# Reading attention's units on an expert-routed decoder trunk: one fused instruction for bias and maximum, factors by pairs, four logit banks, and unread TensorE products in waits

## What is computed

```python
lc = einsum(q, k_cmp) + bias;  pc = masked_softmax(lc)            # 15 compressed blocks
ls = einsum(q, k_slc) + bias;  ps = masked_softmax(ls)            # selected blocks
lw = einsum(q, k_win) + bias;  pw = masked_softmax(lw)            # window
out = g0 * (pc @ v_cmp) + g1 * (ps @ v_slc) + g2 * (pw @ v_win)   # gates per head
h = h + out @ w_out
logits = rmsnorm(h) @ w_router;  top_v, top_i = top_k(logits, 2)
h = h + sum over experts of gate_e * swiglu_e(rmsnorm(h))
```

## Time and profile before

| | us |
|---|---|
| time, median of 3 runs | 1418.52 (1417.91 to 1419.12) |
| profiled execution | 1417.83 |
| its span | 1416.2 |
| PE busy | 1368.9 (97%) |
| DVE busy | 430.5 (30%) |
| ACT busy | 306.0 (22%) |
| POOL busy | 148.9 (11%) |
| mean granted PE clock | 0.986 of full |

### The profile page before, as it was taken

How to read it: one execution, slowest core, us unless ns; L and a number is a source line. 1 busy time by engine, 2 the same in 40 slices (tenths; PEclk the granted TensorE clock), 3 DMA queues, 4 the chain that set the end, 5 groups by cost and what they waited for, 6 DMA issues and landing times.

```text
span 1416.2 us, 36112 instructions
## 1 busy us (share of the span) xinstructions
PE 1368.9 (97%) x16162; PEld 841.7 (59%) x16162; DVE 430.5 (30%) x621; ACT 306.0 (22%) x491; POOL 148.9 (11%) x223
## 2 busy tenths in 40 slices
PE   8999999999998889999999999999999999999995
PEld 7999999998985573453453443444344344344343
DVE  6986555556458730110110110110110110110120
ACT  6735534434457820000000000000000000000000
POOL 0600100000304714001001001001001001001001
PEclk9999999999998999999999999999999999999998
DMA  9853465555957079999999999999999999999993
GB/s 289 257 175 120 129 220 187 180 179 161 187 185 252 28 283 377 400 418 400 419 418 401 418 418 402 418 418 398 419 418 400 418 418 402 418 416 400 406 387 127
DMA packets 132305, 452.08 MB, mean 319 GB/s; under 512 B 12563, under 2 KB 74236, under 8 KB 132162
## 3 DMA queue, kind: packets, MB, share of 16 engines
q1 hardware_dynamic: 126386, 435.11, 79.3%
q0 software_dynamic: 5600, 14.62, 4.2%
q10 hardware_dynamic: 176, 0.14, 0.0%
HBM read 436.46 MB, written 11.80 MB: 317 GB/s over the span
## 4 chain that ended last, share of the span: by engine, by line
PE 93%; DVE 3%; ACT 2%; DMA 1%; issue 1%; POOL 1%; SPq 0%; POOLq 0%; ACTq 0%; DVEq 0%
PE ps L1691 92%; DVE arena L1522 1%; DVE arena L1525 1%; DMA ring<-in_a_w_in 1%; ACT x_hi L964 1%; POOL arena L826 0%; DMA arena<-item_rows,arena 0%; PE ps L1995 0%; ACT arena L1174 0%; ACT x_hi L994 0%; DVE w_lo L527 0%; PE ps L1803 0%; ACT w_hi L521 0%; ACT between L1201 0%; PE ps L1870 0%
## 5 line engine op out<-in xcount | busy, mean ns | idle before, releaser
L1691 PE MATMUL ps<-ring,arena 128*32 128x448 f32 (+1 forms) x3136 | 300.2, 536 | 1.6 <-DVE arena L1650 1.6
L1660 DVE TENSOR_TENSOR arena<-arena,ps 128x448 f32<-128x448 f32 x48 | 29.8, 621 | 755.1 <-PE ps L1691 751.0
L1691 PEld LDWEIGHTS ps<-ring,arena 128*32 128x32 f32 (+1 forms) x3136 | 104.4, 110 | 191.3 <-issue 185.5
L1691 PE MATMUL ps<-more,arena 128*32 128x448 f32 x1920 | 183.3, 539 | 0.0
L527 DVE TENSOR_TENSOR w_lo<-ring,w_hi 128x2048 fp32r<-128x2048 f32 x66 | 151.3, 2295 | 76.9 <-ACT w_hi L521 76.7
L1691 PE MATMUL ps<-more,between 128*32 128x256 f32 x2688 | 158.1, 379 | 0.0
L521 ACT ACTIVATE w_hi<-ring 128x2048 fp32r<-128x2048 f32 x66 | 125.7, 1910 | 93.2 <-PE ps L1691 88.2
L1691 PEld LDWEIGHTS ps<-more,arena 128*32 128x32 f32 x1920 | 62.6, 110 | 115.2 <-issue 113.8
L1691 PEld LDWEIGHTS ps<-more,between 128*32 128x32 f32 x2688 | 92.6, 110 | 53.2
L1245 ACT ACTIVATE arena<-ps 128x448 f32<-128x448 f32 x48 | 26.1, 544 | 413.2 <-PE ps L1691 413.2
L1691 PE MATMUL ps<-x_hi,w_hi 128*128 128x256 f32 x672 | 94.4, 291 | 7.0 <-ACT x_hi L964 5.0
(11 more groups left out here) (279 smaller groups left out, 1376.1 us busy)
## 6 DMA issues: line engine op xcount, KB each, us to landing
ring<-in_moe_w_gu SPq DMA_DIRECT2D x128, 896.0 KB, 19.9
more<-in_moe_w_gu SPq DMA_DIRECT2D x80, 896.0 KB, 19.7
more<-in_moe_w_down SPq DMA_DIRECT2D x64, 896.0 KB, 20.3
arena<-in_moe_w_down SPq DMA_DIRECT2D x32, 896.0 KB, 20.5
ring<-in_ffn_w_gu SPq DMA_DIRECT2D x22, 1024.0 KB, 5.0
ring<-in_a_w_in SPq DMA_DIRECT2D x16, 1024.0 KB, 11.5
silu_g<-in_moe_w_gu SPq DMA_DIRECT2D x16, 896.0 KB, 19.0
xn<-in_moe_w_gu SPq DMA_DIRECT2D x16, 896.0 KB, 19.7
```

What stands on the lines that cost most here:

```text
L1660: dve.tensor_tensor(SU[:, a, :], SU[:, a, :], ps[:, b, 0:QUARTER], ALU.mult).then_inc(bank_free[b], 1)
L1691: return pe.matmul(o, w, x, start=start, stop=stop, **kw)
```

## The change

In attention: one instruction (`tensor_tensor_reduce`) for each branch of a unit adds the bias, negates, and gives the minimum as second output; the exponential uses scale -1 to undo the sign. The exponential of the first branch may start when that branch is done. The factors are computed for two units at once, two units later than before (steps 3, 5, ...). DVE scales the first branch of every unit, POOL the second. From unit 8 on (HB // 2) the logits rotate over four banks, (4, 0, 1, 7)[u % 4]. The compressed branch of the second tile comes at step 8 instead of 12, in bank 6. And `pass_time` issues products of the identity with ones, 256 columns each, into a bank that the next job overwrites: 1, 2, 2, 3 and 3 of them at attention's start, 2 and 2 in the router.

```diff
--- before.py
+++ after.py
@@ -57,6 +57,7 @@
 BUCKETS, MAXDIST = 32, 2048
 COPIES = 16
 NEG = -1e30
+HUGE = 3.0e38
 
 E, ED = 8, 3584
 EK = ED // P
@@ -145,10 +146,6 @@
 def turned_with(u):
 
     return u - u % 2 if ORDER[u // HB] == 0 else u
-
-
-def both_on_pool(u):
-    return ORDER[u // HB] == 0 or u % 2 == 1
 
 
 def job_table():
@@ -214,11 +211,14 @@
     job(("kc",), 7)
     job(("vc",), 6)
     job(("kcsum",), 5)
-    for tt in ORDER:
-        job(("LC", tt), 7)
-        job(("PCT", tt), 7)
     for u in range(TT * HB):
-        job(("L", u), (0, 1, 4)[u % 3])
+        if u in (0, HB):
+            job(("LC", ORDER[u // HB]), 7 - u // HB)
+            job(("PCT", ORDER[u // HB]), 7 - u // HB)
+        if u < HB // 2:
+            job(("L", u), (0, 1, 4)[u % 3])
+        else:
+            job(("L", u), (4, 0, 1, 7)[u % 4])
         if turned_with(u) == u:
             job(("PT", u), 2 + (u // 2 if ORDER[u // HB] == 0 else u) % 2)
     for n in range(TT * 2):
@@ -609,7 +609,7 @@
             b, k = JTURN[name]
             return b, JBASE[b] + k + i * JPER[b]
 
-        CMP_AT = [4 + HB // 2 * ORDER.index(tt) for tt in range(TT)]
+        CMP_AT = [4 + HB // 4 * ORDER.index(tt) for tt in range(TT)]
         units = [(tt, h) for tt in ORDER for h in range(HB)]
 
         def pv_release(eng, u):
@@ -820,10 +820,9 @@
                 pool.dma_start(by_parity(KT, high, br, 0), by_parity(KT, low, br, 0)).then_inc(keys_copied, 16)
 
             for u, (tt, h) in enumerate(units):
-                pool.wait_ge(weight_ready, u + 1)
-                for br in (0, 1) if both_on_pool(u) else (1,):
-                    v = LB[:, u % KEPT, br, 0:P * (tt + 1)]
-                    pool.tensor_scalar(v, v, RW[:, u, br:br + 1], None, ALU.mult).then_inc(p2_ready, 1)
+                pool.wait_ge(weight_ready, u // 2 + 1)
+                v = LB[:, u % KEPT, 1, 0:P * (tt + 1)]
+                pool.tensor_scalar(v, v, RW[:, u, 1:2], None, ALU.mult).then_inc(p2_ready, 1)
 
             pool.wait_ge(counted, 1)
             steps = [0]
@@ -1168,10 +1167,13 @@
             for s in range(len(units) + LAG):
                 if s < len(units):
                     w = P * (units[s][0] + 1)
-                    act.wait_ge(row_max, s + 1)
                     for br in range(2):
+                        if br == 0:
+                            act.wait_ge(row_max, s + 1)
+                        else:
+                            evacuated(act, ("L", s))
                         v = LB[:, s % KEPT, br, 0:w]
-                        act.activation(v, v, ACT.Exp, bias=RM[:, s, br:br + 1], accum_out=RS[:, s, br:br + 1]).then_inc(exp_done, 1)
+                        act.activation(v, v, ACT.Exp, bias=RM[:, s, br:br + 1], scale=-1.0, accum_out=RS[:, s, br:br + 1]).then_inc(exp_done, 1)
                 if s == 0:
                     k = filled(act, ("kcsum",))
                     act.activation(kcsq, ps[:, k, 0:G * NCMP], ACT.Ln, bias=eps[:, :], scale=1.0 / DH).then_inc(bank_free[k], 1)
@@ -1183,11 +1185,6 @@
                     tt = CMP_AT.index(s)
                     act.wait_ge(pc_shift, ORDER.index(tt) + 1)
                     act.activation(PC[:, tt, :, :], PC[:, tt, :, :], ACT.Exp).then_inc(pc_exp, 1)
-                if 1 <= s <= len(units) and not both_on_pool(s - 1):
-                    u = s - 1
-                    act.wait_ge(weight_ready, u + 1)
-                    v = LB[:, u % KEPT, 0, 0:P * (units[u][0] + 1)]
-                    act.activation(v, v, ACT.Copy, scale=RW[:, u, 0:1]).then_inc(p_ready, 1)
                 if s >= LAG:
                     u = s - LAG
                     if units[u][0]:
@@ -1518,11 +1515,13 @@
                 k = filled(dve, ("L", s))
                 if s >= KEPT:
                     filled(dve, ("PT", turned_with(s - KEPT)))
-                lb = LB[:, s % KEPT, :, 0:w]
-                dve.tensor_tensor(lb, ps[:, k, 0:2 * w].rearrange("p (b t) -> p b t", b=2),
-                                  BD[:, h:h + 1, T - w:T].to_broadcast([P, 2, w]), ALU.add).then_inc(bank_free[k], 1)
-                evacuated(dve, ("L", s))
-                dve.reduce_max(RM[:, s, :], lb, AX.X, negate=True).then_inc(row_max, 1)
+                for br in range(2):
+                    last = dve.tensor_tensor_reduce(LB[:, s % KEPT, br, 0:w], ps[:, k, w * br:w * br + w], BD[:, h, T - w:T], -1.0, HUGE,
+                                                    ALU.add, ALU.min, RM[:, s, br:br + 1])
+                    if br == 0:
+                        last.then_inc(row_max, 1)
+                    else:
+                        last.then_inc(bank_free[k], 1)
 
             dve.wait_ge(bias_in, 16 * P // COPIES)
             for n in range(3):
@@ -1557,7 +1556,7 @@
                                               K("seen")[:, tt:tt + 1], wt, ALU.mult, ALU.mult))
                 dve.tensor_tensor(pc, pc, wt.unsqueeze(2).to_broadcast([P, HB, NCMP]), ALU.mult).then_inc(pc_ready, 1)
 
-            for s in range(len(units) + 1):
+            for s in range(len(units) + 2):
                 if s - 3 in CMP_AT:
                     tt = CMP_AT.index(s - 3)
                     k = filled(dve, ("PCT", tt))
@@ -1587,12 +1586,17 @@
                     cmp_scores(CMP_AT.index(s))
                 if s - 1 in CMP_AT:
                     cmp_weights(CMP_AT.index(s - 1))
-                if s >= 1:
-                    u = s - 1
+                if s >= 3 and s % 2 == 1:
+                    u = s - 3
                     tt, h = units[u]
-                    dve.wait_ge(exp_done, 2 * u + 2)
-                    link(dve.reciprocal(RW[:, u, :], RS[:, u, :]))
-                    dve.tensor_tensor(RW[:, u, :], RW[:, u, :], gates[:, tt, 3 * h + 1:3 * h + 3], ALU.mult).then_inc(weight_ready, 1)
+                    dve.wait_ge(exp_done, 2 * u + 4)
+                    link(dve.reciprocal(RW[:, u:u + 2, :], RS[:, u:u + 2, :]))
+                    by_head = gates[:, tt, 3 * h:3 * h + 6].rearrange("p (n b) -> p n b", b=3)
+                    dve.tensor_tensor(RW[:, u:u + 2, :], RW[:, u:u + 2, :], by_head[:, :, 1:3], ALU.mult).then_inc(weight_ready, 1)
+                    dve.wait_ge(weight_ready, u // 2 + 1)
+                    for n in range(2):
+                        v = LB[:, (u + n) % KEPT, 0, 0:P * (tt + 1)]
+                        dve.tensor_scalar(v, v, RW[:, u + n, 0:1], None, ALU.mult).then_inc(p_ready, 1)
             pv_release(dve, len(units) - 3)
             input_lo(OT)
             dve.wait_ge(rows_set, 16 * (E + 2 * T // TILE))
@@ -1984,10 +1988,8 @@
 
             def turned(u):
                 tt = units[u][0]
-                scaled = [both_on_pool(x) for x in range(u + 1)]
-                if scaled.count(False):
-                    pe.wait_ge(p_ready, scaled.count(False))
-                pe.wait_ge(p2_ready, u + 1 + scaled.count(True))
+                pe.wait_ge(p_ready, u + 1)
+                pe.wait_ge(p2_ready, u + 1)
                 b = free_bank(pe, ("PT", u)) if turned_with(u) == u else J[("PT", turned_with(u))][0]
                 for br in range(2):
                     for s in range(tt + 1):
@@ -2028,15 +2030,22 @@
                         last = mm(ps[64 * s:64 * s + G * NCMP, b, 0:HID], RC[:, s, CMP // 4 * half + k, :], w[s][:, k, :],
                                   half == 0 and k == 0, half == 1 and k == CMP // 4 - 1, skip_group_check=True)
                 last.then_inc(w1_used if half == 0 else bank_full[b], 1)
+            def pass_time(job, n):
+
+                b = free_bank(pe, job)
+                for _i in range(n):
+                    mm(ps[:, b, 0:T], ident, ones[:, 0:1].to_broadcast([P, T]), True, True)
+                return b
+
             pe.wait_ge(keys_copied, 16 * 4)
             scores(0)
+            b = pass_time(("hidT",), 1)
             evacuated(pe, ("hid",))
-            b = free_bank(pe, ("hidT",))
             for m in range(2):
                 last = pe.transpose(ps[:, b, P * m:P * m + BOTH], GB[0:BOTH, P * m:P * m + P], ident[0:BOTH, 0:BOTH])
             last.then_inc(bank_full[b], 1)
+            b = pass_time(("kc",), 2)
             pe.wait_ge(gelu_done, 2)
-            b = free_bank(pe, ("kc",))
             for m in range(2):
                 last = mm(ps[:, b, 0:G * NCMP], w2[:, 0, m, :, :].rearrange("p a d -> p (a d)"), GH[:, m, :], m == 0, m == 1)
             last.then_inc(bank_full[b], 1)
@@ -2046,8 +2055,8 @@
                 for m in range(2):
                     last = mm(ps[0:ROWS_C, b, DH * a:DH * a + DH], GHV[:, m, ROWS_C * a:ROWS_C * a + ROWS_C], w2[:, 1, m, 0, :], m == 0, m == 1)
             last.then_inc(bank_full[b], 1)
+            b = pass_time(("kcsum",), 2)
             pe.wait_ge(sq_b, 3)
-            b = free_bank(pe, ("kcsum",))
             mm(ps[:, b, 0:G * NCMP], halves, kcsq, True, True).then_inc(bank_full[b], 1)
             for br in (1, 2):
                 evacuated(pe, ("v", br))
@@ -2060,6 +2069,10 @@
```

(5 more changed lines are left out.)

## The result

The changed kernel takes 1411.98 us (median of five executions, 1410.24 to 1413.79) against 1418.91 us (1417.91 to 1419.92) for the kernel before: a ratio of 0.994, 95% interval 0.9924 to 0.9956, so 7 us faster. The profiled execution took 1410.24 us, with a span of 1408.5 and a mean granted PE clock of 0.993 (before 1417.83, 1416.2 and 0.986). It is the fastest of its five; the one of before lies just under the lowest of its five (1417.91), so the profiles stand at the low end of both sets.

The account below looks back on a forecast made before the run. PE bounds the expert stage, so only its start moves: 2.4 + 2.5 + 1.3 + 1.5 + 2.5 = 10.2 us off 1417.83 gives 1407.6, with 0.7 for the median 1408.3 us. Range, 8 in 10: 1403.5 to 1414.

Parts of the forecast that it names:

- First units: Attention's start to the scores of unit 8: these come at 442.9 instead of 445.31, a gain of 2.4 us.
- they lie where PE idles: Attention's first units: fills sit in PE's idle times of 0.4 to 1 us, delaying unit 2's scores by a hidden 0.4.
- the walk: Step-by-step timing through attention; at its start PE waits at 436.7 for factors and issues unit 8's scores at 442.9.
- rival (1): First units and router: the fill doesn't hold PE's clock; 1412.8 us with both lost, about 1410.5 with one; chance 0.17.
- Wide units: Attention's 256-key units, scores 8 to 20: PE paces, six pairs take 24.1 us against 26.6, a gain of 2.5.
- Narrow units: Attention's 128-key units, scores 20 to 30: five pairs take 11.3 us against 12.54, a gain of 1.3.
- now ACT and PE pace at 2.25: Narrow pairs after the change: ACT and PE set 2.25 us a pair, where POOL had set 2.51.
- Tail: End of attention: POOL's last eight scalings become four, a gain of 1.5 us.
- Router: Ahead of the experts: 48 gather products take 2.7 us at full clock instead of 5.38, a gain of 2.5.
- Rival (2): Attention's scalings: DVE and POOL block each other, up to 0.75 us on DVE per pair; 1411.8 us; chance 0.11.
- Rival (3): Attention's fused instruction is paced by its own feedback, up to 1581 ns each; 1445 us; chance 0.07, including another wait.
- Rival (4): Expert stage: weight transfers bound it once it starts 10 us earlier; no gain beyond attention's, or none, 1418; chance 0.03.

Follow-up runs that it names:

- e4: Changed kernel with four more unread products around the transposition of the compressed weights and the router's second fill ahead of the bank wait; 1410.79 us, ratio 0.9939.
- e8: Changed kernel with DVE scaling only 2 columns of the first branch, the rest unscaled; one execution, 18.45 us from scores of unit 0 to 8.
- e1: Changed kernel without any of its fifteen unread products; 1414.46 us, ratio to before 0.9968.
- e5: Kernel before the change with the fused bias and maximum alone; 1413.18 us, ratio to before 0.9946.
- e6: Changed kernel with add and maximum as two instructions again; 1421.75 us, ratio to before 1.001.
- e10: Changed kernel with factors for each unit alone and scaling by POOL and ACT as before; 1411.07 us, ratio to before 0.9945.
- e13: Changed kernel with ACT copying only a quarter of the narrow units' transposed rows; one execution, 11.70 us from scores of unit 20 to 30.

## Why the prediction was right, and where its numbers failed

**Direction, mechanism and range** held: faster, by parts in the places named, with an experts' stage of unchanged length, and 1411.98 lies inside 1403.5 to 1414. But it lies above the forecast's own range (1404.5 to 1411) and in that of the clock lost in one place or both (1409.5 to 1413.5), and this is what happened, in one place. The point, 1408.3, is 3.7 too low: 2.6 of that are the terms, and 1.0 that the median lies 1.74 above the profiled execution, where I had added 0.7 from before.

**First units, 2.4 against 0.94.** This is the term that failed, in the step "they lie where PE idles". I took the fills to hold the clock up to the scores of unit 8, and named the windows 430 to 445; but the last fill is issued at step 4, and the walk itself has PE waiting at 436.7 for factors. PE did wait, from 437.5 to 439.8 with small pieces between, and no fill lay there. That is rival (1) in one half of one place. e4 shows that with the clock held the stretch gains 2.36. That this meets 2.4 so closely is partly luck: two of my prices were off and cancel. DVE's pair was to be 4 x 0.42 for the fused instructions and 0.5 for the scalings; measured it is 4 x 0.34 and 0.84, 2.2 us either way; narrow it was 4 x 0.29 and 0.3 against 4 x 0.21 and 0.60, 1.45 either way. Apart from POOL a wide scaling takes 0.35, my upper bound, and not 0.25. DVE's scalings cost 0.58 us in this stretch (e8 against e4), and without fill the whole of the change brings it 0.05 (e1).

**Wide units, 2.5 against 2.44.** Right in size; e5 and e6 put it on the fused instruction. The wait in it was named wrongly: I put 1.8 us of waiting for POOL there, and the trace shows 1.07 us for DVE's scaling, up to 451.78, and 0.42 for POOL, up to 463.09. Start to start the fused instruction is 0.34 us with its read (from 434.11 to 434.45 in the changed kernel), 0.21 narrow, against my 0.42 and 0.29: the cheaper end of the bounds. The rule of the Trainium skill that I cited, in "VectorE: DVE Perf Modes", section "Two Vector instructions with no wait between them", agrees in form: the trace shows an accumulator read behind each one. The saving beyond my price bought nothing, as far as these rows show, since PE paces these pairs, as I said: 3.33 us from 454.49 to 457.82.

**Narrow units, 1.3 against 0.84.** Here the reason was half wrong though the sign was right. "POOL bounds them" was right in the sum for the old factors: e10's last pairs run at POOL's 2.32, and what it hasn't done by then is paid behind them. The step that failed is what comes next, "now ACT and PE pace at 2.25". e13 takes ACT's load out. As the timelines show it, the pace is the loop of 2.31 us a pair above. I had said that the factors' wait costs nothing, because they stand behind later biases: the wait is indeed short, but standing behind the biases is itself a part of the loop.

**Tail, 1.5 against 0.95.** The path is the one I named: the chain of waits goes from the last exponentials over the factors at 482.56 and DVE's scaling at 482.97 to the transposes at 483.28. Only its length, which I gave without a working, was off by 0.55.

**Router, 2.5 against 2.46.** Right, and for the reason given: gather products in 2.80 us instead of 5.38, where 2.7 was predicted. I put the delay by the fills at 0.1; it is some 0.2 (e4). How much of the gain needs the fill varies: 1.3 against e1, 2.2 against e5.

**Rival (2), blocking,** is there with 0.22 us on DVE per wide pair and 0.11 per narrow one, not with 0.75. The product of two columns beside POOL's 1024 columns still takes 910 ns in the changed kernel, so that row was true of its own case and not of a scaling beside a scaling. The page "SBUF — State Buffer", section "Who interferes with whom", of the Trainium skill says that the second engine fully blocks when a DVE instruction uses both pairs of ports, which it says a scaling can do. By the measurement it does not, for these shapes: DVE's second scaling, started while a POOL instruction of 1.08 us runs, takes 0.57 instead of 0.35. Whether DVE's scaling used both pairs no view shows. **Rival (3),** the feedback, is out: 0.34. **Rival (4),** the weights, is out: 867.23 us at 412 GB/s, eight us earlier.

## What to carry to other kernels

Unread products hold the clock only as far as they reach: here two waits close together behind the last one lost it again, and four more products, or shorter waits, kept it. Look at windows of 1 us behind the last one, and put fills ahead of waits that are certain, never between a wait that ends and the work it releases. An engine that is nearly always busy need not be the pace (ACT, 93% of the window), and one can set it only after a lead is used up (POOL in e10): follow one pair round through every engine, and see what stands in front of each step in its queue. An instruction that merges two passes may pay mainly by the room it makes for work that would otherwise not fit. And before pricing an edit by a stretch, look at the granted clock in both kernels: much of e8's and e10's difference in one stretch was clock.

## What the hardware showed that was not expected

- The fused add, scale and minimum over 256 columns, read from PSUM, takes 417 ns, no more than the plain add of 256 columns did before (421 ns); the carried minimum costs only the read, 82 ns, which overlaps with the next instruction. The scan's 1581 ns are no guide to it.
- After two waits of 0.77 and 1.07 us within 2.3 us the granted clock went to the lower level from about 440.3 to 443.7, although PE was busy again by then: the products behind the wait pay, not the wait. Behind waits of 0.28 and 1.00 us in the same place (e8) and behind one of 1.07 alone (at 451.78) it stayed at 1.00; behind two of 0.73 us at the end of attention (e5, e10) it fell.
- Of two DVE scalings issued together with two of POOL, only the second of DVE (568 instead of 348 ns) and the first of POOL (1082 instead of 924) are longer than apart; a mean over both shows 0.11 and 0.05 us and no pattern.
- Five unread products some 80 us ahead of attention, in a wait of 2.5 us, brought 1.2 to 2.0 us up to the scores of unit 0 (79.27 against 80.5 to 81.3).
